# Regrouping the start-up loads of a hybrid encoder step, moving thirteen tiny loads into the convolution stage, and walking the first weight slab by row tile

## The reference

```python
sc = jax.nn.silu(c)
mod = (sc @ p['ada_w'][l] + p['ada_b'][l])[:, None, :]
sh_m, sc_m, gt_m, sh_f, sc_f, gt_f = jnp.split(mod, 6, axis=-1)
h = _rmsnorm(x, p['pre_mix_g'][l]) * (1 + sc_m) + sh_m
proj = h @ w_in                       # 4096 columns and 16 for the gates
xp = jnp.concatenate([conv_ctx, qkv], axis=1)
conv = sum(xp[:, i:i + T] * conv_w[i] for i in range(4))
qkv_c = jax.nn.silu(conv)
```

## Time and profile before

| | us |
|---|---|
| median of 3 runs | 1863.98 (1863.34 to 1864.18) |
| the profiled execution's own time | 1860.38 |
| its span | 1858.7 |
| PE busy | 1636.5 (88%) |
| DVE busy | 1152.2 (62%) |
| ACT busy | 972.4 (52%) |
| DMA, mean over the span | 227 GB/s |

### The profile page before, as it was taken

How to read it: one execution, slowest core, us unless ns; L and a number is a source line. 1 busy time by engine, 2 the same in 40 slices (tenths; PEclk the granted TensorE clock), 3 DMA queues, 4 the chain that set the end, 5 groups by cost and what they waited for, 6 DMA issues and landing times. The chain is left out here.

```text
span 1858.7 us, 26541 instructions
## 1 busy us (share of the span) xinstructions
PE 1636.5 (88%) x10764; PEld 1393.8 (75%) x10764; DVE 1152.2 (62%) x1222; ACT 972.4 (52%) x1147; POOL 45.0 (2%) x148
## 2 busy tenths in 40 slices
PE   3699789956999995987775999999999999999992
PEld 2699366645999994986575888888888888888882
DVE  1685251144444334344634788889897989888883
ACT  1443422245433335332544777767776777677771
POOL 2121010000000000000000000000000000000000
PEclk8899799978999997999886999999999999999996
DMA  8640859663454343323020899999998999999970
GB/s 252 212 116 11 317 185 352 249 183 102 122 151 151 127 154 114 114 79 115 1 91 1 307 371 354 345 321 357 364 364 305 354 363 359 330 332 374 352 283 31
DMA packets 260582, 421.29 MB, mean 227 GB/s; under 512 B 12167, under 2 KB 125008, under 8 KB 260432
## 3 DMA queue, kind: packets, MB, share of 16 engines
q1 hardware_dynamic: 254352, 415.55, 65.2%
q10 hardware_dynamic: 6092, 3.90, 0.8%
HBM read 414.34 MB, written 5.07 MB: 226 GB/s over the span
## 5 line engine op out<-in xcount | busy, mean ns | idle before, releaser
L2532 DVE TENSOR_TENSOR w_lo_late<-raw,w_hi_late 128x2048 fp32r<-128x2048 f32 x264 | 600.7, 2289 | 93.7 <-ACT w_hi_late L2464 92.1
L2464 ACT ACTIVATE w_hi_late<-raw 128x2048 fp32r<-128x2048 f32 x264 | 505.3, 1918 | 172.9 <-PE bank L352 172.9
L350 PE MATMUL bank<-w_hi_late,hg_hi 128*128 128x512 f32 (+1 forms) x768 | 290.3, 378 | 1.2 <-DVE w_lo_late L2532 0.5
L352 PE MATMUL bank<-w_hi_late,hg_lo 128*128 128x512 f32 (+1 forms) x768 | 286.0, 372 | 0.0
L351 PE MATMUL bank<-w_lo_late,hg_hi 128*128 128x512 f32 (+1 forms) x768 | 285.6, 372 | 0.0
L271 DVE TENSOR_TENSOR w_lo_main<-raw,w_hi_main 128x2048 fp32r<-128x2048 f32 (+1 forms) x50 | 112.3, 2250 | 118.4 <-ACT w_hi_main L264 118.3
L350 PEld LDWEIGHTS bank<-w_hi_late,hg_hi 128*128 128x128 f32 x768 | 144.7, 188 | 31.7 <-DVE w_lo_late L2532 7.4
L352 PEld LDWEIGHTS bank<-w_hi_late,hg_lo 128*128 128x128 f32 x768 | 144.6, 188 | 25.8
L351 PEld LDWEIGHTS bank<-w_lo_late,hg_hi 128*128 128x128 f32 x768 | 144.8, 189 | 24.0
L350 PE MATMUL bank<-w_hi_late,act_hi 128*128 128x512 f32 x352 | 138.3, 393 | 0.0
L352 PE MATMUL bank<-w_hi_late,act_lo 128*128 128x512 f32 x352 | 137.2, 390 | 0.0
(11 more groups left out here) (463 smaller groups left out, 2873.0 us busy)
## 6 DMA issues: line engine op xcount, KB each, us to landing
raw<-in_moe_w_gate SPq DMA_DIRECT2D x88, 1024.0 KB, 6.9
raw<-in_moe_w_up SPq DMA_DIRECT2D x88, 1024.0 KB, 7.2
raw<-in_moe_w_down SPq DMA_DIRECT2D x88, 1024.0 KB, 7.2
ada_delta<-in_ada_w SPq DMA_DIRECT2D x40, 1024.0 KB, 8.7
raw<-in_gdn_w_in SPq DMA_DIRECT2D x16, 1024.0 KB, 6.7
raw<-in_ffn_w_gate SPq DMA_DIRECT2D x22, 512.0 KB, 4.0
raw<-in_ffn_w_up SPq DMA_DIRECT2D x22, 512.0 KB, 5.3
ada_start<-in_ada_w SPq DMA_DIRECT2D x8, 1024.0 KB, 14.4
```

Source lines behind the costliest of these rows:

```text
L350: pe.matmul(out, w_hi, x_hi, start=start, stop=False)
L352: return pe.matmul(out, w_lo, x_hi, start=False, stop=stop)
L2464: act.activation(k.w_hi[:, m % SPL, :], k.raw[:, m % RAW, :], ACT.Copy).then_inc(k.hi_ready, 1)
L2532: dve.tensor_tensor(k.w_lo[:, m % SPL, :], k.raw[:, m % RAW, :], k.w_hi[:, m % SPL, :], ALU.subtract).then_inc(k.raw_split, 1)
```

## The change

1. **Groups.** The eleven loads of `first` become two groups. The condition rows and the gains, eight loads, go first and have a semaphore of their own (`rows_in`); the three of the input rows follow (`first_in`). PE and ACT wait for each where they use it, and PE takes two `ada` pieces ahead of turning the input rows and two behind it.
2. **Tiny loads.** Thirteen loads (`wba`, `wlf`, the router's, the biases, the gate vectors) leave ACT's queue. SP issues them in the convolution stage, between slab 9 and slab 10, and the gates stage waits for them.
3. **Slabs.** The setup loads slabs 0, 1 and 2 only, slab 0 ahead of the eighth `ada` piece; the convolution stage loads the others.
4. **First split.** ACT and DVE split slab 0 in the setup. ACT makes the high part of slab 1 before the last row tile's. The input rows use the memory of `y_tok`, and the squares go to a buffer of their own, with a wait between them.
5. **First slab.** Where `x_ready` is given, `dense_tiles` takes both column halves of a row tile before the next row tile, in the first slab only.

```diff
-        first, loads = [], []
+        conds, first, loads, late = [], [], [], []
...
         @block.sync
         def _(sp):
-            for n in range(ADA_GROUP):
+            for n in range(ADA_GROUP - 1):
                 k.ada_load(sp, n)
-            for n in range(RAW):
+            k.load(sp, 0)
+            k.ada_load(sp, ADA_GROUP - 1)
+            for n in range(1, 3):
                 k.load(sp, n)
...
             pe.wait_ge(const_ready, 1)
+            pe.wait_ge(rows_in, 16 * len(conds))
+            turn(0)
+            pe.wait_ge(cond_ready, 1)
+            k.ada_pe(pe, 2)
             pe.wait_ge(first_in, 16 * len(first))
-            for n in range(n_first):
+            for n in range(1, n_first):
                 turn(n)
-            pe.wait_ge(cond_ready, 1)
-            k.ada_pe(pe, 4)
+            k.ada_pe(pe, 2)
...
             for dst, src in loads:
                 act.dma_start(dst, src).then_inc(small_in, 16)
-            act.wait_ge(first_in, 16 * len(first))
             act.wait_ge(copied, 1)
...
             last.then_inc(cond_ready, 1)
+            act.wait_ge(first_in, 16 * len(first))
...
             act.activation(ss[:], ss[:], ACT.Exp, scale=-0.5).then_inc(root, 1)
+            k.ahead_hi(act, 0)
             k.ada_act(act, 4)
...
             dve.wait_ge(copied, len(turns))
+            k.ahead_lo(dve, 0)
             k.ada_dve(dve, 4)
...
-        for half in range(2):
-            tile = 2 * group + half
-            if g == 0:
-                bank_free(tile)
...
+        steps = [(half, q) for half in range(2) for q in range(n_k[g])]
+        if x_ready is not None and s == 0:
+            steps = [(half, q) for q in range(n_k[g]) for half in range(2)]
...
-            for n in range(n0 + RAW, n0 + n_slabs):
+            for n in range(n0 + 3, n0 + n_slabs):
+                if n == n0 + RAW + 4:
+                    for dst, src in k.late:
+                        sp.dma_start(dst, src).then_inc(k.late_in, 16)
                 k.load(sp, n)
...
                 act.activation(h_hi[:, kt, :], h32[:, kt, :], ACT.Copy).then_inc(hi_done, 1)
+                if kt == KT - 2:
+                    k.ahead_hi(act, n0 + 1)
             k.ahead_hi(act, n0 + AHEAD - 1)
...
+            pe.wait_ge(k.late_in, 16 * len(k.late))
```

More of the change, by code:

```diff
@@ L379, in setup_phase @@
     nc, i = k.nc, k.i
[L380 removed]
+    x_tok = k.y_tok
+    with nc.sbuf_tensor("row_squares", [P, D], F32) as row_squares, \
             nc.sbuf_tensor("rows_a", [112, P], F32) as rows_a, \
@@ L396, in early, with cond, other @@
             first.append((dst, src))
-        early(rows_b[73:81], i["c_prompt"].rearrange("o (r c) -> (o r) c", c=P))
-        early(rows_b[81:89], i["c_sample"].rearrange("o (r c) -> (o r) c", c=P))
+        def cond(dst, src):
+            conds.append((dst, src))
+        def other(dst, src):
+            late.append((dst, src))
+        cond(rows_b[73:81], i["c_prompt"].rearrange("o (r c) -> (o r) c", c=P))
+        cond(rows_b[81:89], i["c_sample"].rearrange("o (r c) -> (o r) c", c=P))
         for t in range(2):
@@ L493, in _ @@
             run = k.act_chain.on(act)
+            for dst, src in conds:
+                act.dma_start(dst, src).then_inc(rows_in, 16)
             for dst, src in first:
@@ L503, in _ @@
             last.then_inc(cond_ready, 1)
+            act.wait_ge(first_in, 16 * len(first))
             for t, (t0, nt) in enumerate(TOKEN_TILES):
-                last = act.activation(k.y_tok[0:nt, t, :], x_tok[0:nt, t, :], ACT.Square, accum_out=ss[0:nt, t:t + 1])
+                last = act.activation(row_squares[0:nt, :], x_tok[0:nt, t, :], ACT.Square, accum_out=ss[0:nt, t:t + 1])
+                if t < 2:
+                    run(last)
             run(last)
@@ L758, in dense_tiles @@
         w_lo = k.slab_view(k.w_lo, m % SPL, 0, 256, n_k[g], 256)
-        for half in range(2):
-            tile = 2 * group + half
-            if g == 0:
-                bank_free(tile)
[L763 to L767, removed]
-                last = k.three(pe, banks[tile % len(banks)][:, 0:T], w_hi[:, q, c], w_lo[:, q, c], x_hi[:, kt, :],
-                               x_lo[:, kt, :], start=(kt == 0), stop=(kt == sum(n_k) - 1))
+        if g == 0:
+            bank_free(2 * group)
+            bank_free(2 * group + 1)
+        steps = [(half, q) for half in range(2) for q in range(n_k[g])]
+        if x_ready is not None and s == 0:
+            steps = [(half, q) for q in range(n_k[g]) for half in range(2)]
+        for half, q in steps:
+            tile, kt, c = 2 * group + half, sum(n_k[:g]) + q, slice(half * P, (half + 1) * P)
+            if x_ready is not None and s == half == 0:
+                x_ready(kt)
+            last = k.three(pe, banks[tile % len(banks)][:, 0:T], w_hi[:, q, c], w_lo[:, q, c], x_hi[:, kt, :],
+                           x_lo[:, kt, :], start=(kt == 0), stop=(kt == sum(n_k) - 1))
         last.then_inc(k.split_read, 1)
@@ L2685, in build @@
         k.conv_cols = early.enter_context(nc.sbuf_tensor("conv_cols", [P, QKV_T, 7], F32))
+        split = ctx.enter_context(ExitStack())
+        k.split_buffers(split, "in")
         right = ctx.enter_context(ExitStack())
@@ L2705, in build @@
                     h_hi, h_lo = parts(s, "h_mix0")
-                    with ExitStack() as split:
-                        k.split_buffers(split, "in")
-                        conv_phase(k, h32, h_hi, h_lo, qkv, z_silu, last_rows)
+                    conv_phase(k, h32, h_hi, h_lo, qkv, z_silu, last_rows)
+                    split.close()
                     ring = gdn.enter_context(ExitStack())
```

24 lines of the change are left out of this document (13 added, 11 removed).

## The result

The changed kernel takes **1822.7 us** (median of 4 runs, 1820.95 to 1824.18) against 1863.66 for the kernel before in the same comparison: ratio 0.978, 95% interval 0.9764 to 0.9798. The forecast was 1839.8 with a range from 1835 to 1848. The profiled execution took 1820.95, its span is 1819.2, against 1860.38 and 1858.7.

A forecast was written before the change was run, and what follows sets the result against it. The convolution stage, where PE is always busy, and the serial front end before it were taken as the bound; gains of 13.5 (setup), 10.0 (first slab) and 0.7 (later stages) took 1863.98 to 1839.8 us, range 1835 to 1848.

The forecast's parts named there:

- Whatever ends earlier ahead of that stage ends the whole kernel earlier; whatever speeds up something inside it does nothing.: Opening claim about the convolution stage, where PE is busy for 20.00 of 20.00 us; no size of its own.
- The gain is taken back: Rival: something unseen, such as a later stage at a lower clock, leaves the time within 0.2%, 1864 us; chance 0.03.
- Sum: Whole kernel: gains of 13.5, 10.0 and 0.7 us make 24.2, so the median 1863.98 becomes 1839.8 us.
- Part 1: Setup: earlier `c_pad` keeps the weight stream unbroken; convolution stage starts at 39.6, not 53.1; gain 13.5 us, bounds 11.0 to 15.0.
- Part 1, small transfers: Setup's DMA stream: ACT's small packets cost it nothing, 343 GB/s beside them against 348 without.
- When the eighth `ada` piece lands: Setup: this landing sets the setup's length; taken as 35.8 us, between 34.5 by bytes and 37.0 by landings.
- Part 2: Convolution stage's first slab: slab 1 begins 13.2 us into the stage instead of 23.2; gain 10.0 us, bounds 8 to 10.8.
- Part 3: other stages: First slabs of three later stages: interleaving fills PE's gaps, 0.2 to 0.4 us each; together 0.7 us, bounds 0 to 1.5.
- Part 4: the moved loads: Convolution stage: slabs and tiny loads issued by SP there stay hidden, with 10 us left; cost 0.
- The low clock: Rival: PE stays at low clock through the setup's gaps and starts slab 1 low; 1855.0 us, chance 0.07.
- The blocked queue: Rival: tiny loads block SP's queue ahead of slab 10; 1875 us at three times the measured price, chance 0.02.
- the late condition rows: Rival in the setup: condition rows land much after 16, so the seventh piece stays late; 8 us lost, 1847.8 us, chance 0.07.

## Why the prediction was wrong, step by step

- **"Whatever ends earlier ahead of that stage ends the whole kernel earlier; whatever speeds up something inside it does nothing."** The first half holds: 24.7 us of lead at the end of the convolution, 24.7 at the last expert. The sum then took the rest of the kernel as unchanged. **That is the step that failed:** it lacks a term of 14.8 us for the end (41.0 to 26.2). In the rival "The gain is taken back" I wrote that all later stages "have no date of their own, so I find no place for it". I looked for waits between engines and for transfers; a cost that depends on where an instruction lies in the program is neither. It was to be seen: 18.47 us without work behind the last expert, ended by a barrier, with ten instruction packets beside it. I had read the trace only to 190 us.
- **Sum.** 13.5 + 10.0 + 0.7 = 24.2; the front gave 24.7. The parts are 14.7, then 10.3 up to the start of slab 1; 0.3 of it was gone by the end of the stage. Part 1's lower bound adds up to 10.8 (53.1 - 37.0 - 3.5 - 1.8), not 11.0.
- **Part 1: groups and tiny loads.** Right in mechanism and order, 1.2 us too cautious (38.40, not 39.6). The split of this part, from the runs: tiny loads 11.6; three slabs 1.7, the hold that was left in that kernel (2.06 - 0.32), or 2.5 by the kernel with six slabs; groups, the order on SP and the rest 1.4 by difference, not tested alone, and no more than two executions of one front differ by. I had given the groups much of the argument, and by this they matter least.
- **Part 1, small transfers.** I went by the rate, 343 GB/s with the small packets beside 348 without, and gave their removal nothing. The changed kernel moves 386 and 365 GB/s in these stretches. I had compared with one row, and others without small packets show 375 and 355. So the one row could not show that the small packets cost the stream nothing; how much of the 1.2 us is due to them no run shows, since what else is queued has changed as well.
- **When the eighth `ada` piece lands.** Forecast 35.8; PE's last wait for it ends at 35.0, the byte count's bound.
- **Part 2: the first slab.** Right: 2.46, 11.9, 1.05 and 12.9 against 2.3, 11.8, 1.3 and 13.2. It is one gain of three edits: take away the early split and all of it is gone, take away the interleaving and 4.1 of it is gone. When the clock comes back did not matter: in the seven kernels with both, 3.1 to 6.0 us after PE's start, slab 1 begins 10.4 us after that start each time.
- **Part 3: other stages.** Gained where it was looked for, and gone at the end. PE's first slab takes 8.4 us instead of 10.3 in the up projection and 8.9 instead of 9.4 in the key projection. The lead is 24.7 at the start of the SwiGLU, 26.6 at the end of the up projection, 25.1 at the end of the down projection, 25.5 at the end of the key projection, and 24.5 at the query projection. Much of this goes with the clock: in the up projection's first slab the full clock is there after 3.0 us instead of 6.2, and at the start of the down projection the changed kernel has 0.60 and 0.54 granted from 600 to 604 us where the kernel before has 1.00 (626 to 630). Where the clock comes back after 6.2 us as before (with one idle instruction, and with the rounds left out), the up projection's first slab takes 9.9: 0.4 gained, as forecast. From the start of the SwiGLU to the last expert the lead goes from 24.7 to 24.7, and with one, two and 129 idle instructions from 23.1 to 23.2, 21.3 to 22.6 and 24.6 to 24.5. What ends last in the attention was not looked into.
- **Part 4: the moved loads.** Cost 0, as said. The thirteen issues took 13.2 us on SP (56.1 to 69.3), not the 22.4 they took on ACT, and no engine waits for a slab in the stage.
- **Rivals.** The low clock did not come where it was priced: the normed rows took 5.97 us. It came behind them, 0.53 granted from 31 to 34 us while PE read the fifth and the sixth `ada` piece, and cost nothing, since the eighth landed at 35.0. The blocked queue and the late condition rows (8.99) are refuted. None of them ended below the range.

## What to carry to other kernels

Read the end of the trace as carefully as the place of the edit: a barrier that ended a wait of 18.47 us with no arithmetic and no data DMA, and ten instruction packets beside it, was code being fetched here. With this loop over some 900 DVE instructions, one instruction of 60 ns more shifted the time by 14.5 us; where a trace ends like this one, test a step with one idle instruction more before believing or rejecting a change, and don't walk empty rounds (without them the end was 18.9 us shorter before and 4.1 after). Loads that nobody needs yet cost most where they stand ahead of the first arithmetic in an engine's own program (11.6 us here), then where a barrier has to wait for their issue (2.5 us).

## What the runs showed of the hardware that I had not expected

- One DVE instruction of 60 ns, placed some 1600 us ahead of the loop's end, made the kernel 14.5 us slower or 15 us faster. DVE's jumps at the loop's foot and head took 3.3 to 3.7 us in the kernel before, and in the changed one 2.9 us the first time and 0.3 to 0.4 us after it. The packets beside them are 8 KB each, and the long end of the foot at 1886 (40.8 us) came back with the foot at 2014 (41.0 us), 128 instructions on.
- PE's full clock came back 3.3 us after its start in the changed kernel's first slab, and 5.5 us after it before the change; I had reckoned with 5.5. Over all runs it is 3.1 to 6.0 us with the changed first slab, 3.5 to 6.2 with the old one or without the early split, and 12.7 us in the run without interleaving, where PE issues 7 matmuls in 2 us (42 to 44) instead of 9.
- Executions of the same front differ by 1 to 3 us where the first stage ends: the changed kernel begins its convolution stage at 38.40, 39.12 and 39.73 with 0, 2 and 1 idle instructions, which stand behind it, and the kernel before at 53.10, at 54.33 with the rounds left out and at 55.84 with one. So the two executions compared above are both among the earliest of their kind. A part worth 1 us has to be read from its mechanism, not from one pair of profiles.
